# Reading the weight columns of each product as four quarters by turns

## The chip, the cores and the metric

The program runs on one core of one Trainium2 chip. The metric is the device time of one execution in microseconds (us). A core has a matrix engine (PE, whose loads of the stationary operand are shown apart as PEld), a vector engine (DVE), a scalar engine (ACT), GpSimd (POOL) and a queue engine (SP), which work side by side and wait for each other by semaphores.

## The reference

Two transformer-like blocks of depth one are computed one after the other on 256 rows of 2048 numbers, all in float32. Cut to its large products:

```
h    = rmsnorm(x) * (1 + sc_a) + sh_a          # sc_a, sh_a, ... = silu(c) @ w_ada + b_ada
proj = h @ w_in                                # 2048 x 6144; then rope, dilated and differential attention
x    = x + gt_a * rmsnorm(mix @ w_out)         # 2048 x 2048
f    = (silu(h @ w_gate) * (h @ w_up)) @ w_down
x    = x + gt_f * rmsnorm(f)
# second block
proj = h @ w_in_2 + b_in_2                     # mLSTM in chunks, a causal convolution, gates
merged = sigmoid(g_a) * (h_a @ w_proj_a_2) + sigmoid(g_b) * (h_b @ w_proj_b_2)
x    = x + gate * (merged @ w_out_2)
```

## The kernel before

The rows of the activations are the stationary operand, two tiles of 128 rows, transposed beforehand so that the contraction lies on the partitions. The weights stream through as the moving operand. They are arranged on the host into chunks of 128 partitions x 2048 float32, each a contiguous row per partition. The SP queue brings one chunk per DMA into RAW. The stages are named first (w_in and w_out), ffn (w_gate and w_up), down (w_down) and second (all weights of the second block). Chunks of the two modulation matrices (w_mod) are mixed in between; they are not used as matrix products, DVE multiplies and sums them (L1638).

Float32 products of full precision are built from three cheaper ones. A chunk is used in two halves of 1024 columns. For each half ACT rounds RAW to the type fp32r and writes it to HI (L669), DVE writes the rest, RAW minus HI, to LO (L1628). The activations stand likewise as XH and XL. PE then sums XH x HI, XL x HI and XH x LO in PSUM. A product with operands of type fp32r passes once through the array ("one-pass product"); a product with plain float32 operands is shown in the trace as two records, each of which takes longer. Every one-pass product of the weights has a stationary operand of 128 x 128 and 512 moving columns:

- `products` (L1181 with HI, L1186 with LO) serves ffn and down: for each half 8 products with HI and 4 with LO.
- `narrow_high` (L1197, L1198) and `narrow_low` (L1206) serve first and second: again 8 and 4 for a half.
- `narrow_direct` (L1221) takes some halves of the first stage as plain float32, from WHOLE, so that neither HI nor LO is needed. These halves are chosen by `is_direct`.

HI and LO have four slots of one half each (HLS = 4). PE's last product of a half raises half_used, which allows ACT to write that slot again. The order of work on each engine is written out by hand; the queues hold to it.

At the start, PE has little to do. It runs idle products on a square of ones (`run_warm`, L1282), 22 behind the products that spread c over the partitions (L1289), and 14 behind the first transposes (L1261), before the first real products of the weights (L1221). Results of these idle products are overwritten.

Of the kernel before, what the change touches and what calls it, by code (L numbers as in the profile page):

```python
# [22 lines left out]
F32 = mybir.dt.float32  # L23
# [7 lines left out]
P = 128  # L31
# [9 lines left out]
NKF = D_FF // P  # L41
# [12 lines left out]
HLS = 4  # L54
# [23 lines left out]
W_IN_COLS = [3072, 4096, 3584, 4608, 5120, 5632, 0, 1024, 512, 1536, 2048, 2560]  # L78
# [19 lines left out]
def first_half(h):  # L98

    if h < 8 * EARLY:  # L100
        n, g = divmod(h, EARLY)
    else:
        g, n = divmod(h, 8)
    return g, n, n == 0, n == 7
# [6 lines left out]
def is_direct(h):  # L111
    if h >= 8 * EARLY:
        return False
    g, n, *_ = first_half(h)
    return g in DIRECT and n < DIRECT_PAIRS
# [248 lines left out]
def build(nc, x, c_rows, pos_cols, smalls, lambda_q1, lambda_k1, lambda_q2, lambda_k2,  # L364
# [4 lines left out]
    with ctx:  # L369
# [8 lines left out]
        PS = ctx.enter_context(nc.psum_tensor("PS", [P, 8, 512], F32))  # L378
        RAW = sb("RAW", [P, RAWS, 2048])
        HI = sb("HI", [P, HLS, 1024], F32R)  # L380
        LO = sb("LO", [P, HLS, 1024], F32R)
# [127 lines left out]
        s = namedtuple("Semaphores", names)(*[sem(n) for n in names])  # L509
# [28 lines left out]
        def as_it_is(h):  # L538

            n, g = divmod(h, EARLY)  # L540
            return WHOLE[:, (n * len(DIRECT) + DIRECT.index(g)) % 4, :]

        def bank_of(g):
            return 2 * (g % 2)
# [628 lines left out]
        def _(pe):  # L1173
            def products(ready, slot, slot_k, bank_of, first, last, rows=range(NT)):

                pe.wait_ge(s.hi_ready, ready)
                for u in rows:
                    xh, xl = (v[:, slot_k, u * P:(u + 1) * P] for v in (XH, XL))
                    for x in (xh, xl):
                        for cc in range(2):  # L1180
                            pe.matmul(PS[:, bank_of(u, cc), :], x, HI[:, slot, cc * 512:(cc + 1) * 512],  # L1181
                                      start=first and x is xh, stop=False)
                pe.wait_ge(s.lo_ready, ready)
                for u in rows:
                    for cc in range(2):
                        m = pe.matmul(PS[:, bank_of(u, cc), :], XH[:, slot_k, u * P:(u + 1) * P],  # L1186
                                      LO[:, slot, cc * 512:(cc + 1) * 512], start=False, stop=last)
                return m

            def narrow_high(sec, h, n, bank, start, us):  # L1190

                pe.wait_ge(s.hi_ready, sec.half(0, h) + 1)
                for kk in range(2):
                    hi = HI[:, h % HLS, kk * 512:(kk + 1) * 512]
                    for u in us:
                        rows = slice(u * P, (u + 1) * P)
                        pe.matmul(PS[:, bank + u, :], XH[:, 2 * n + kk, rows], hi, start=start and kk == 0, stop=False)  # L1197
                        pe.matmul(PS[:, bank + u, :], XL[:, 2 * n + kk, rows], hi, start=False, stop=False)  # L1198

            def narrow_low(sec, h, n, bank, stop, us):  # L1200

                pe.wait_ge(s.lo_ready, sec.half(0, h) + 1)
                for kk in range(2):
                    lo = LO[:, h % HLS, kk * 512:(kk + 1) * 512]
                    for u in us:
                        m = pe.matmul(PS[:, bank + u, :], XH[:, 2 * n + kk, u * P:(u + 1) * P], lo, start=False,  # L1206
                                      stop=stop and kk == 1)
                if 1 in us:
                    m.then_inc(s.half_used, 1)
                return m  # L1210
# [68 lines left out]
            def run_warm(bank, count):  # L1279

                for _ in range(count):
                    pe.matmul(PS[:, bank, 0:P], ONES_SQUARE, ONES_SQUARE, start=True, stop=True)  # L1282

            pe.wait_ge(s.dve_chain, 2)
            run_warm(7, 9)
            pe.wait_ge(s.c_silu, 1)
            for n in range(2):
                for b in (2 * n, 2 * n + 1):
                    m = pe.matmul(PS[:, b, :], ONES_SQUARE, C_ROW[:, 512 * b:512 * b + 512], start=True, stop=True)  # L1289
                m.then_inc(s.c_spread, 1)  # L1290
            run_warm(7, 22)
            pe.wait_ge(s.small_in, 16)
            pe.wait_ge(s.cact_ready, 1)
            pe.wait_ge(s.xn_0, 1)
# [3 lines left out]
            for k in range(NK):  # L1298
                m = turn(1, k)
                if k % 4 == 3:  # L1300
                    m.then_inc(s.src_t, 1)
            pe.wait_ge(s.xt_out, 1)
            run_warm(0, 14)
            pe.wait_ge(s.xt_out, 4)

            used = [0]
# [125 lines left out]
            for h in range(sec.n_halves):  # L1432
                if h < 96:
                    g, n, start, stop = first_half(h)
                    bank = first_bank(g)
# [12 lines left out]
                else:  # L1448
                    g, k = W_OUT_CHUNKS[(h - 96) // 2]
                    n = 2 * k + h % 2  # L1450
                    bank = 2 if h // 4 in (25, 27, 29) else 0
                    start, stop = h in (96, 100, 104, 116, 120), h in (99, 111, 115, 119, 127)
# [12 lines left out]
                if h == sec.n_halves - 4:  # L1465

                    for i in range(4):
                        m = narrow(sec, h + i, n + i, bank, False, i == 3, (0,))
# [29 lines left out]
            for it in sec.items:  # L1498
                if it["kind"] != "W":
                    continue  # L1500
                g, k = it["what"]
                q = g % 2
                for hf in range(2):
                    h = it["half"] + hf
# [94 lines left out]
            for h in range(2, HALVES_2):  # L1599
                g, n = divmod(h, 8)  # L1600
# [6 lines left out]
                if h == HALVES_2 - 4:  # L1607

                    for i in range(4):
                        m = narrow(sec, h + i, n + i, bank_of(g), False, i == 3, (0,))  # L1610
# [6 lines left out]
        def _(dve):  # L1617
            link = chain(dve, s.dve_chain)
# [213 lines left out]
            link(dve.memset(ONES_SQUARE, 1.0))  # L1832
            link(dve.memset(C_ROW, 0.0))
            link(dve.memset(GATE_COL, 0.0))
            dve.wait_ge(s.cact_ready, 1)
            sec = secs["first"]

# [246 lines left out]
            for it in sec.items:  # L2084
# [14 lines left out]
                for hf in range(2):  # L2099
                    h = it["half"] + hf  # L2100
# [15 lines left out]
            for it in sec.items:  # L2116
# [3 lines left out]
                g = it["what"][0]  # L2120
# [314 lines left out]
def laid_out(inputs):  # L2435

    w = {name: np.asarray(inputs[name])[0] for name in ("w_ada", "w_ada_2", "w_in", "w_out", "w_gate", "w_up", "w_down", "w_in_2",
                                                        "w_proj_a_2", "w_proj_b_2", "w_out_2")}

    def rows(v, k, n):  # L2440

        return v[k * P:(k + n) * P].reshape(n, P, -1).transpose(1, 0, 2)

    def chunks(pieces):
        return np.stack([np.concatenate(p, axis=2).reshape(P, 2048) for p in pieces])


    turned = [w[name].T.reshape(-1, P, D) for name in ("w_ada", "w_ada_2")]

    def in_turn(a, b):  # L2450

        return np.concatenate([np.stack([a[0:NK], a[NK:2 * NK]], axis=1).reshape(-1, *a.shape[1:]), a[2 * NK:], b])

    def first():
        for n in range(16):
            yield [np.concatenate([rows(w["w_in"][:, W_IN_COLS[g]:W_IN_COLS[g] + 512], 2 * k, 2)
                                   for g, k, *_ in (first_half(2 * n), first_half(2 * n + 1))], axis=1)]
        for n in range(16, 48):
            g, k, _, _ = first_half(2 * n)
            yield [rows(w["w_in"][:, W_IN_COLS[g]:W_IN_COLS[g] + 512], 2 * k, 4)]  # L2460
        for g, k in W_OUT_CHUNKS:
            yield [rows(w["w_out"][:, 512 * g:512 * g + 512], 4 * k, 4)]

    def ffn():
        for g in range(11):
            for k in range(0, NK, 2):
                yield [rows(w[name][:, 512 * g:512 * g + 512], k, 2) for name in ("w_gate", "w_up")]

    def second():
        for g in range(GROUPS_2):  # L2470
            name, at = source_of(g)
            for k in range(0, NK, 4):
                yield [rows(w[name][:, at:at + 512], k, 4)]

    def columns(*vectors):
        return np.concatenate([np.asarray(v).reshape(-1, P).T for v in vectors], axis=1)

    b_ada, b_ada_2 = (np.asarray(inputs[name])[0].reshape(-1, P) for name in ("b_ada", "b_ada_2"))
    return {"w_mod": in_turn(*turned), "w_first": chunks(first()), "w_ffn": chunks(ffn()),
            "w_down": w["w_down"].reshape(NKF, P, 2048), "w_second": chunks(second()),  # L2480
            "w_gates": rows(w["w_in_2"][:, GATES_AT:GATES_AT + 16], 0, NK).reshape(P, 16 * NK),
            "b_gates": np.asarray(inputs["b_in_2"])[0, GATES_AT:GATES_AT + 16].reshape(16, 1),
            "c_rows": np.concatenate([np.asarray(inputs[n]).reshape(1, D) for n in ("c", "c_2")]), "pos_cols": np.asarray(inputs["positions"]).reshape(NT, P).T,
            "smalls": np.concatenate([columns(*(inputs[n] for n in ("g_pre_attn", "g_pre_ffn", "norm1_w_2", "conv_w_2", "headnorm_w_2", "g_out_a",
                                                  "g_subln_b", "g_post_attn", "g_post_ffn"))),
                                      in_turn(b_ada, b_ada_2).T, np.eye(P), np.repeat(inverse_frequencies(), P, axis=0)],
                                     axis=1).astype(np.float32)}
# [37 lines left out]
```

## Time and profile before

| | us |
|---|---|
| median of 2 runs | 2366.81 (2366.06 to 2367.56) |
| profiled execution, first to last instruction (span) | 2365.2 |
| median less the span: what lies around it | 1.6 |
| PE busy | 2335.2 (99% of the span) |
| DVE busy | 1816.7 (77%) |
| ACT busy | 1121.5 (47%) |

The profiled execution is given by its span alone, so the sums are made on the span and 1.6 us is added. A busy share says how much of the span an engine had an instruction in work; PE's records overlap, since a product's record reaches from its entry to the end of its results, and the next product enters before that. The distance from one start to the next is what a product costs in a row of them.

### The profile page before, as it was taken

The numbers are of one execution on the slowest core, as the hardware profiler recorded it, in microseconds if no ns is written. First come the engines' busy times: TensorE is split into PE (matmuls) and PEld (weight loads), VectorE is DVE, ScalarE is ACT, GpSimd is POOL, SyncE is SP. The second block draws the span as 40 slices with busy tenths as digits, with TensorE's granted clock in tenths as the row PEclk, the third lists the DMA queues.
The fourth block names the chain that finished last, engine by engine and source line by source line (L and its number), as shares of the span: only waits on it lengthen the run. The fifth ranks groups of instructions, "written<-read, shape, count | busy, mean of one in ns | idle before, by whom it ended". The sixth has DMA issues, their size and how long they took to land.

```text
span 2365.2 us, 26320 instructions
## 1 busy us (share of the span) xinstructions
PE 2335.2 (99%) x10346; PEld 1891.5 (80%) x10346; DVE 1816.7 (77%) x2447; ACT 1121.5 (47%) x1473; POOL 14.8 (1%) x31
## 2 busy tenths in 40 slices
PE   8999999999999999999999999999999999999998
PEld 5377788788888888888878888888888888888887
DVE  6788988888888888978575577997877795555775
ACT  5355676554434444444464334444345544444453
POOL 0000000000000000000000000000000000000000
PEclk9999999999999999999999999999999999999999
DMA  9987889887788777888646555555555556555553
GB/s 398 420 294 282 309 320 336 305 320 284 282 305 307 281 280 279 313 333 318 248 157 213 199 191 195 192 194 206 204 206 204 200 203 251 204 196 192 184 195 124
DMA packets 87758, 598.48 MB, mean 253 GB/s; under 512 B 10145, under 2 KB 10209, under 8 KB 16593
## 3 DMA queue, kind: packets, MB, share of 16 engines
q1 hardware_dynamic: 85538, 588.95, 68.7%
q0 software_dynamic: 1664, 7.19, 0.9%
q8 instruction: 82, 1.34, 0.2%
q10 hardware_dynamic: 432, 0.66, 0.1%
q14 instruction: 42, 0.34, 0.0%
HBM read 594.62 MB, written 2.13 MB: 252 GB/s over the span
## 4 chain that ended last, share of the span: by engine, by line
PE 90%; DVE 4%; DMA 4%; ACT 1%; issue 1%; DVEq 0%; ACTq 0%
PE PS L1181 19%; PE PS L1197 19%; PE PS L1198 19%; PE PS L1206 19%; PE PS L1186 10%; DMA RAW<-in_w_mod 2%; DVE RAW L1638 2%; DMA RAW<-in_w_first 1%; DVE LO L1628 1%; PE PS L1333 1%; PE PS L1552 0%; DVE X L1719 0%; DMA RAW<-in_w_ffn 0%; PE PS L1322 0%; ACT HI L669 0%
## 5 line engine op out<-in xcount | busy, mean ns | idle before, releaser
L669 ACT ACTIVATE HI<-RAW 128x1024 fp32r<-128x1024 f32 x784 | 828.7, 1059 | 1101.2 <-PE PS L1206 695.2
L1628 DVE TENSOR_TENSOR LO<-RAW,HI 128x1024 fp32r<-128x1024 f32 x784 | 957.4, 1224 | 462.3 <-ACT HI L669 458.5
L1197 PE MATMUL PS<-HI,XH 128*128 128x512 f32 x2080 | 821.8, 395 | 2.8 <-ACT HI L669 1.9
L1198 PE MATMUL PS<-HI,XL 128*128 128x512 f32 x2080 | 810.5, 390 | 0.0
L1206 PE MATMUL PS<-LO,XH 128*128 128x512 f32 x2080 | 558.4, 389 | 1.8 <-DVE LO L1628 1.8
L1197 PEld LDWEIGHTS PS<-HI,XH 128*128 128x128 f32 x2080 | 390.5, 188 | 87.4 <-DVE XL L1900 3.0
L1206 PEld LDWEIGHTS PS<-LO,XH 128*128 128x128 f32 x2080 | 390.2, 188 | 84.6 <-DVE LO L1628 2.9
L1198 PEld LDWEIGHTS PS<-HI,XL 128*128 128x128 f32 x2080 | 390.7, 188 | 78.9
L1181 PE MATMUL PS<-HI,XH 128*128 128x512 f32 x1056 | 325.9, 390 | 1.7 <-DVE XL L1742 1.1
L1181 PE MATMUL PS<-HI,XL 128*128 128x512 f32 x1056 | 325.2, 389 | 0.0
L1186 PE MATMUL PS<-LO,XH 128*128 128x512 f32 x1056 | 283.9, 389 | 0.0
L1638 DVE CUSTOM_DVE_ANT_0 RAW<-RAW,BIAS 128x2048 f32<-128x2048 f32 x96 | 219.3, 2288 | 31.9 <-DMA RAW<-in_w_mod 24.1
L1670 DVE STREAM_TRANSPOSE R<-R 32x256 f32<-32x256 f32 (+1 forms) x608 | 230.7, 379 | 12.7
L1181 PEld LDWEIGHTS PS<-HI,XH 128*128 128x128 f32 x1056 | 197.6, 188 | 43.1 <-DVE XL L1742 1.8
L1181 PEld LDWEIGHTS PS<-HI,XL 128*128 128x128 f32 x1056 | 198.1, 188 | 41.4
L1186 PEld LDWEIGHTS PS<-LO,XH 128*128 128x128 f32 x1056 | 198.1, 188 | 41.4 <-DVE LO L1628 0.2
L1638 DVE CUSTOM_DVE_ANT_0 RAW<-RAW,R 128x2048 f32<-128x2048 f32 x48 | 109.9, 2289 | 0.5
L1221 PE MATMUL PS<-R 128*128 128x512 f32 x192 | 86.9, 607 | 8.5 <-ACT R L666 5.2
L1221 PEld LDWEIGHTS PS<-R 128*128 128x128 f32 x192 | 36.2, 193 | 58.5 <-issue 51.9
L666 ACT ACTIVATE R<-RAW 128x1024 f32<-128x1024 f32 x24 | 24.1, 1048 | 49.2 <-DMA RAW<-in_w_first 49.2
L2321 DVE TENSOR_TENSOR R<-PS,BIAS 128x1024 f32<-128x1024 f32 x24 | 29.2, 1217 | 0.0
L727 ACT ACTIVATE R<-PS,MOD,SCALE 128x256 f32<-128x256 f32 (+1 forms) x38 | 17.9, 521 | 4.4 <-PE PS L1270 4.3
(263 smaller groups left out, 886.9 us busy)
## 6 DMA issues: line engine op xcount, KB each, us to landing
RAW<-in_w_second SPq DMA_DIRECT2D x208, 1024.0 KB, 4.9
RAW<-in_w_mod SPq DMA_DIRECT2D x144, 1024.0 KB, 5.6
RAW<-in_w_ffn SPq DMA_DIRECT2D x88, 1024.0 KB, 4.9
RAW<-in_w_first SPq DMA_DIRECT2D x64, 1024.0 KB, 5.3
RAW<-in_w_down SPq DMA_DIRECT2D x44, 1024.0 KB, 5.0
BIAS<-in_b_in SPq DMA_DIRECT2D x40, 256.0 KB, 5.1
R<-mod_rows POOLq DMA_DIRECT2D x3, 1024.0 KB, 7.9
X<-in_x SPq DMA_DIRECT2D x2, 1024.0 KB, 8.7
```

Source lines behind the costliest of these rows:

```text
L666: act.activation(as_it_is(h), whole, ACT.Copy).then_inc(s.hi_ready, 1)
L669: act.activation(HI[:, (it["half"] + hf) % HLS, :], whole, ACT.Copy).then_inc(s.hi_ready, 1)
L1181: pe.matmul(PS[:, bank_of(u, cc), :], x, HI[:, slot, cc * 512:(cc + 1) * 512], start=first and x is xh, stop=False)
L1186: m = pe.matmul(PS[:, bank_of(u, cc), :], XH[:, slot_k, u * P:(u + 1) * P], LO[:, slot, cc * 512:(cc + 1) * 512], start=False, stop=last)
L1197: pe.matmul(PS[:, bank + u, :], XH[:, 2 * n + kk, rows], hi, start=start and kk == 0, stop=False)
L1198: pe.matmul(PS[:, bank + u, :], XL[:, 2 * n + kk, rows], hi, start=False, stop=False)
L1206: m = pe.matmul(PS[:, bank + u, :], XH[:, 2 * n + kk, u * P:(u + 1) * P], lo, start=False, stop=stop and kk == 1)
L1221: m = pe.matmul(PS[:, bank + u, :], XT[:, 2 * n + kk, u * P:(u + 1) * P], as_it_is(h)[:, kk * 512:(kk + 1) * 512], start=start and kk == 0 ...
L1628: dve.tensor_tensor(LO[:, slot, :], RAW[:, it["slot"], hf * 1024:(hf + 1) * 1024], HI[:, slot, :].bitcast(F32), ALU.subtract).then_inc(s.l ...
L1638: dve.tensor_tensor_reduce(w, w, C_ROW if a < ADA_OF_C else C_ROW_2, 1.0, 0.0, ALU.mult, ALU.add, MOD[:, a:a + 1]).then_inc(s.ada_step, 1)
L1670: m = dve.transpose(columns(b, a), rows(a, b))
L2321: dve.tensor_tensor(dst, y, bias, ALU.add).then_inc(s.group_out, 1)
```

## The change

1. On the host, each group of 512 columns of the weights that are read by one-pass products is arranged anew (`by_fours`): columns 0, 4, 8, ..., 508 come first, then 1, 5, 9, ..., then 2, 6, ..., then 3, 7, .... The halves that `narrow_direct` reads stay as they were. Sizes and number of the DMAs are the same, and so is the work of ACT and DVE on them, element by element.
2. In `products`, `narrow_high` and `narrow_low` PE reads the 512 moving columns through `by_turns`: the first element of each of the four quarters of 128, then the second of each, and so on. Within a partition consecutive reads lie 512 bytes apart, where they lay 4 bytes apart. Since the two permutations undo each other, PSUM receives the columns in their true order.
3. The 22 idle products at first are replaced by 20 one-pass products on HI slot 3 filled with ones (`first_warm`), and the 14 by 16 others (`second_warm`). They read their moving operand in several strided orders; four of the 16 are on plain float32. A memset of that slot on DVE is added for them, and PE waits for it.

```diff
+        def by_turns(v):
+            return v.rearrange("p (a b) -> p b a", a=4)
...
-                            pe.matmul(PS[:, bank_of(u, cc), :], x, HI[:, slot, cc * 512:(cc + 1) * 512],
+                            pe.matmul(PS[:, bank_of(u, cc), :], x, by_turns(HI[:, slot, cc * 512:(cc + 1) * 512]),
                                       start=first and x is xh, stop=False)
...
-                                      LO[:, slot, cc * 512:(cc + 1) * 512], start=False, stop=last)
+                                      by_turns(LO[:, slot, cc * 512:(cc + 1) * 512]), start=False, stop=last)
...
-                    hi = HI[:, h % HLS, kk * 512:(kk + 1) * 512]
+                    hi = by_turns(HI[:, h % HLS, kk * 512:(kk + 1) * 512])
...
-                    lo = LO[:, h % HLS, kk * 512:(kk + 1) * 512]
+                    lo = by_turns(LO[:, h % HLS, kk * 512:(kk + 1) * 512])
...
+            def warm(m, n, count, a, b, bank=7):
+                for _ in range(count):
+                    pe.matmul(PS[0:m, bank, 0:n], a, b, start=True, stop=True)
+
+            def first_warm():
+                v = HI[:, 3, :]
+                x = v[:, 0:P]
+                warm(P, 512, 4, x, v[:, 0:512].rearrange("p (a b) -> p b a", a=4))
+                warm(P, 512, 4, x, v[:, 0:512].rearrange("p (a b) -> p b a", a=8))
+                warm(P, 512, 4, x, v.rearrange("p (a b) -> p b a", a=2)[:, 0:256, :])
+                warm(P, 256, 4, x, v[:, 0:256].rearrange("p (a b) -> p b a", a=2))
+                warm(P, 512, 4, x, by_turns(v[:, 0:512]))
+
+            def second_warm():
+                v = HI[:, 3, :]
+                x = v[:, 0:P]
+                warm(P, 512, 4, x, v[:, 0:512].rearrange("p (a b c) -> p b a c", a=2, c=2), 0)
+                warm(P, 512, 4, x.bitcast(F32), by_turns(v[:, 0:512]).bitcast(F32), 0)
+                warm(P, 512, 4, x, v[:, 0:512].rearrange("p (a b) -> p b a", a=64), 0)
+                warm(P, 512, 4, x, by_turns(v[:, 0:512]), 0)
...
-            run_warm(7, 22)
+            pe.wait_ge(s.dve_chain, 5)
+            first_warm()
...
-            run_warm(0, 14)
+            second_warm()
...
             link(dve.memset(GATE_COL, 0.0))
+            link(dve.memset(HI[:, 3, :].bitcast(F32), 1.0))
...
+    def by_fours(a):
+        return a.reshape(*a.shape[:-1], -1, P, 4).swapaxes(-1, -2).reshape(a.shape)
...
-            yield [rows(w["w_out"][:, 512 * g:512 * g + 512], 4 * k, 4)]
+            yield [by_fours(rows(w["w_out"][:, 512 * g:512 * g + 512], 4 * k, 4))]
...
-            "w_down": w["w_down"].reshape(NKF, P, 2048), "w_second": chunks(second()),
+            "w_down": by_fours(w["w_down"].reshape(NKF, P, 2048)), "w_second": chunks(second()),
```

PE at the start of the program, before the change: L1282 are the idle products, L1289 spreads c, L1261 are the transposes of x, L1221 the first products of the weights.

```order
L1282 MATMUL PS<-R 128x128 x9
L1289 MATMUL PS<-BIAS,R 128x512 x4
L1282 MATMUL PS<-R 128x128 x22
L1261 MATMUL PS<-SMALLS,R 128x128 x32
L1282 MATMUL PS<-R 128x128 x14
L1221 MATMUL PS<-R 128x512 x96
```

The same place on PE in the changed kernel; there the idle products of `warm` are L1291, and the lines L1289, L1261 and L1221 have become L1317, L1265 and L1225.

```order
L1286 MATMUL PS<-R 128x128 x9
L1317 MATMUL PS<-BIAS,R 128x512 x4
L1291 MATMUL PS<-HI 128x512 x12
L1291 MATMUL PS<-HI 128x256 x4
L1291 MATMUL PS<-HI 128x512 x4
L1265 MATMUL PS<-SMALLS,R 128x128 x32
L1291 MATMUL PS<-HI 128x512 x16
L1225 MATMUL PS<-R 128x512 x96
```

Nothing else is moved: only the idle products in front of the transposes and in front of the first real products are others, and wider.

## Rows read from the trace of the kernel before

**Rows 1.** The page's head: span, and busy time of PE.

```profile
span 2365.2 us, 26320 instructions
...
PE 2335.2 (99%) x10346; PEld 1891.5 (80%) x10346; DVE 1816.7 (77%) x2447; ACT 1121.5 (47%) x1473; POOL 14.8 (1%) x31
```

**Rows 2.** The chain that ended last, by line, shares of the span.

```profile
by line: PE PS L1181 19.5%; PE PS L1197 19.3%; PE PS L1198 19.1%; PE PS L1206 19.1%; PE PS L1186 9.7%; DMA RAW<-in_w_mod 2.2%; DVE RAW L1638 1.5%; DMA RAW<-in_w_first 1.3%; DVE LO L1628 0.7%; PE PS L1333 0.6%; issue 0.5%; PE PS L1552 0.4%; 
```

**Rows 3.** Waits: engine, line, waited for, us in total, times, longest.

```profile
ACT HI L669 <- PE PS L1206: 695.2, 445, 2.9
```

**Rows 4.** Groups of PE's products, shapes apart: busy us, mean ns, idle before.

```profile
L1197 PE MATMUL PS<-HI,XH 128*128 128x512 f32 x2080 | 821.8, 395 | 2.8 <-ACT HI L669 1.9 <-DVE XL L1742 1.0
L1198 PE MATMUL PS<-HI,XL 128*128 128x512 f32 x2080 | 810.5, 390 | 0.0
L1206 PE MATMUL PS<-LO,XH 128*128 128x512 f32 x2080 | 558.4, 389 | 1.8 <-DVE LO L1628 1.8
L1181 PE MATMUL PS<-HI,XH 128*128 128x512 f32 x1056 | 325.9, 390 | 1.7 <-DVE XL L1742 1.1 <-issue 0.6
L1181 PE MATMUL PS<-HI,XL 128*128 128x512 f32 x1056 | 325.2, 389 | 0.0
L1186 PE MATMUL PS<-LO,XH 128*128 128x512 f32 x1056 | 283.9, 389 | 0.0
```

**Rows 5.** The chain in stage down: start us, us, what.

```profile
992.35 1.81 PE PS L1181 x8
994.16 0.91 PE PS L1186 x4
995.07 1.81 PE PS L1181 x8
```

**Rows 6.** Windows: us, busy of PE, PEld, DVE, ACT, POOL, then PEclk, DMA share, GB/s.

```profile
990.00:1000.00 10.00, 10.00 (x46) 8.29 (x45) 9.82 (x13) 4.58 (x6) 0.00 (x0) 1.00 0.94 350
1700.00:1710.00 10.00, 10.00 (x46) 8.29 (x45) 8.65 (x12) 4.43 (x5) 0.00 (x0) 1.00 0.62 210
```

**Rows 7.** The chain in stage second.

```profile
1702.37 0.91 PE PS L1206 x4
```

**Rows 8.** Timeline of PE, one-pass products of 256 columns, 16 stationary columns.

```profile
1226.12 0.28 PE L1525 MATMUL PS<-XH,WIFH 128*16 128x256 f32 x1
...
1226.69 0.28 PE L1525 MATMUL PS<-XH,WIFL 128*16 128x256 f32 x1
1226.81 0.39 PE L1197 MATMUL PS<-HI,XH 128*128 128x512 f32 x1
```

**Rows 9.** Timeline of PEld beside plain float32 products of 512 columns.

```profile
28.72 0.34 PEld L1221 LDWEIGHTS PS<-R 128*128 128x128 f32 x1 [0.52 <-issue]
29.57 0.34 PEld L1221 LDWEIGHTS PS<-R 128*128 128x128 f32 x1 [0.52 <-issue]
...
31.43 0.19 PEld L1221 LDWEIGHTS PS<-R 128*128 128x128 f32 x1 [0.24 <-ACT R L666]
31.86 0.19 PEld L1221 LDWEIGHTS PS<-R 128*128 128x128 f32 x1 [0.24 <-issue]
```

**Rows 10.** Windows of the granted clock, columns as in rows 6.

```profile
27.20:30.70 3.50, 3.50 (x6) 1.44 (x5) 2.68 (x4) 0.45 (x1) 0.00 (x0) 0.51 1.00 424
30.70:34.00 3.30, 3.30 (x8) 1.40 (x8) 1.26 (x1) 1.55 (x2) 0.00 (x0) 1.00 1.02 432
```

**Rows 11.** Windows of longer stretches, columns as in rows 6.

```profile
130.00:290.00 160.00, 157.69 (x739) 125.76 (x738) 142.89 (x262) 92.33 (x202) 1.08 (x2) 1.00 0.80 290
290.00:440.00 150.00, 149.45 (x728) 125.11 (x727) 131.89 (x179) 96.88 (x207) 0.00 (x0) 1.00 0.90 332
760.00:1040.00 280.00, 280.00 (x1237) 231.84 (x1236) 237.40 (x273) 121.12 (x129) 0.00 (x0) 1.00 0.80 293
```

**Rows 12.** Timeline of the start, DVE and PE.

```profile
3.46 0.09 DVE L1834 MEMSET SMALL<- 128x32 f32 x1
...
9.65 5.07 PE L1282 MATMUL PS<-R 128*128 128x128 f32 x44
...
11.02 2.29 DVE L1638 CUSTOM_DVE_ANT_0 RAW<-RAW,BIAS 128x2048 f32<-128x2048 f32 x1 [7.47 <-ACT BIAS L749]
...
15.29 1.94 PE L1261 MATMUL PS<-SMALLS,R 128*128 128x128 f32 x16 [0.56 <-DVE R L1849]
...
20.03 3.37 PE L1282 MATMUL PS<-R 128*128 128x128 f32 x28
```

**Rows 13.** Timeline of PE, its next work behind those idle products.

```profile
26.66 3.98 PE L1221 MATMUL PS<-R 128*128 128x512 f32 x5 [3.26 <-ACT XH L784]
```

More of the change, by code:

```diff
@@ L2452, in in_turn @@
         return np.concatenate([np.stack([a[0:NK], a[NK:2 * NK]], axis=1).reshape(-1, *a.shape[1:]), a[2 * NK:], b])
+    def by_fours(a):
+        return a.reshape(*a.shape[:-1], -1, P, 4).swapaxes(-1, -2).reshape(a.shape)
     def first():
         for n in range(16):
-            yield [np.concatenate([rows(w["w_in"][:, W_IN_COLS[g]:W_IN_COLS[g] + 512], 2 * k, 2)
-                                   for g, k, *_ in (first_half(2 * n), first_half(2 * n + 1))], axis=1)]
+            halves = []
+            for h in (2 * n, 2 * n + 1):
+                g, k, *_ = first_half(h)
+                piece = rows(w["w_in"][:, W_IN_COLS[g]:W_IN_COLS[g] + 512], 2 * k, 2)
+                halves.append(piece if is_direct(h) else by_fours(piece))
+            yield [np.concatenate(halves, axis=1)]
         for n in range(16, 48):
             g, k, _, _ = first_half(2 * n)
-            yield [rows(w["w_in"][:, W_IN_COLS[g]:W_IN_COLS[g] + 512], 2 * k, 4)]
+            yield [by_fours(rows(w["w_in"][:, W_IN_COLS[g]:W_IN_COLS[g] + 512], 2 * k, 4))]
         for g, k in W_OUT_CHUNKS:
-            yield [rows(w["w_out"][:, 512 * g:512 * g + 512], 4 * k, 4)]
+            yield [by_fours(rows(w["w_out"][:, 512 * g:512 * g + 512], 4 * k, 4))]
     def ffn():
@@ L2466, in ffn @@
             for k in range(0, NK, 2):
-                yield [rows(w[name][:, 512 * g:512 * g + 512], k, 2) for name in ("w_gate", "w_up")]
+                yield [by_fours(rows(w[name][:, 512 * g:512 * g + 512], k, 2)) for name in ("w_gate", "w_up")]
     def second():
@@ L2472, in second @@
             for k in range(0, NK, 4):
-                yield [rows(w[name][:, at:at + 512], k, 4)]
+                yield [by_fours(rows(w[name][:, at:at + 512], k, 4))]
     def columns(*vectors):
```

## The prediction

> **What bounds the kernel now.** I read the page's head first: PE is busy for 2335.2 of 2365.2 us [rows 1]. A busy share alone doesn't tell that an engine sets the time, so the chain of waits comes second. By line it is L1181, L1197, L1198, L1206 and L1186, together 86.7% of the span [rows 2]. These are exactly the lines whose moving operand the change reads otherwise. Seen from the other side, ACT spends 695.2 us waiting for PE to release a slot of HI [rows 3], which is what a producer does when the consumer is the bound.
>
> Next comes what one product costs in a row of them, the distance between starts and not the mean of 389 ns in the groups [rows 4], which holds the pipeline too. The chain has 8 products in 1.81 us and 4 in 0.91 us [rows 5]: 1.81 / 8 = 226.3 ns, and one half of 12 products takes 995.07 − 992.35 = 2.72 us, so 226.7 ns each. The granted clock is 1.00 there [rows 6], the 2.4 GHz level, and at one column per cycle 512 columns would take 512 / 2.4 = 213.3 ns. So 13.3 ns of each are over, one part in 16.
>
> **Where the 13.3 ns come from** decides the forecast, and four rows narrow it.
> - It is not traffic: the DMA share is 0.94 in one stretch and 0.62 in the other [rows 6], and the price of 4 products is 0.91 us in both [rows 5, 7].
> - It is no fixed cost for an instruction. The one-pass products of 256 columns start 6 in 1226.81 − 1226.12 = 0.69 us [rows 8], 115 ns each against 106.7 ns of columns: 8 ns over. With half the columns well over half of the excess stays, so I take a part by column and a little by instruction.
> - It is not the load of the stationary operand: those products load 16 columns instead of 128 and have the excess all the same [rows 8].
> - It is gone when columns are taken at half the rate. A record of a plain float32 product of 512 columns takes 31.86 − 31.43 = 0.43 us at the high clock [rows 9, 10], about 2 x 213.3 = 426.7 ns plus some 2 ns. Had the loss been one in 16 there as well, it would be 453 ns.
>
> So what is lost is lost while PE takes 4-byte columns from neighbouring addresses at one per cycle. Either the reader stumbles on neighbouring addresses (one cycle lost for each 64 bytes), which another order may avoid, or it can't deliver more than this of 4-byte elements in any order. No product of the kernel before reads its moving operand with a step, so no row tells which; the price of the new reading has to be bounded from both sides.
>
> **The change, part by part.**
>
> *The reading by turns.* It concerns 3 x 2080 + 3 x 1056 = 9408 products [rows 4]. On the chain they make 86.7% of 2365.2 = 2050.6 us [rows 2], which is 2050.6 / 0.2267 = 9046 of them; the others lie beside other work, mostly in the first 130 us. The best price is the bare 213.3 ns plus the some 2 ns that a float32 record has over its columns [rows 9], an estimate of 215.3 ns. That saves 11.4 ns x 9046 = 103 us, and 107 us if all 9408 count. The lower end without any fixed cost is 13.3 x 9408 = 125 us saved. The worst near price is that of a record that takes columns at half the rate, 0.43 us [rows 9]: 0.203 x 9408 = 1910 us lost. I take the end at 215.3 ns. The reason is the last of the four rows: the loss follows the full rate over neighbouring addresses, not the number of columns, and by turns each of four streams is read at a quarter of the rate. It is a judgement, and the price of being wrong is large.
>
> The Trainium skill has a rule that speaks against this: "Advanced Engine Details and Errata", section "SBUF Cachelines", says that memory is read in lines of 16 bytes, that at least two hits on a line are needed to cover its latency, and that a different line at each access is penalised. By turns every read is in another line than the one before. No row of this trace shows a strided read by PE, so the rule is neither confirmed nor refuted; what it would do is the first rival below. The same skill's "TensorE: Matmul & The Clock Gate", section "Back-to-back issue gap", gives the distance of isolated products as N / 2.4 + 2.5 ns, 215.8 ns for 512 columns; the trace has 226.7. An estimate by that page would save 10.9 x 9046 = 99 us, about what my sum has.
>
> *What the faster PE runs into.* With 215.3 ns a half takes 2.58 us instead of 2.72. DVE is busy for 142.89 of 160 us from 130 on, 131.89 of 150 from 290 on and 237.40 of 280 us in 760 to 1040 [rows 11]. If these stretches shrink by some 4 to 5%, its share goes to 94%, 92% and 89%. It stays below PE, but its work comes in blocks of 2.29 us (L1638) [rows 12] and LO must be there in time. The DMA share in 290 to 440 goes from 0.90 to 0.94. I book 2 us of new waits, between 0 and 12 us.
>
> *ACT and DVE on HI and LO, and the DMAs.* Same sizes, contiguous on their side: nothing.
>
> *The memset on DVE.* It stands behind the one at 3.46 us; DVE then idles 7.47 us until 11.02 for ACT's BIAS [rows 12]. A memset of 1024 columns lies in there. Cost nothing; PE's new wait for it is over before 9.65, where the idle products begin.
>
> *The first idle products.* Before: 44 records in 5.07 us, from 9.65 to 14.7, and the transposes begin at 15.29, since they wait for DVE [rows 12]. Now 16 of 512 and 4 of 256 columns: at 0.215 and 0.11 us that is 3.9 us, done at 13.6. At half the rate 16 x 0.43 + 4 x 0.21 = 7.7 us, done at 17.4, 2 us late.
>
> *The second idle products.* Before: 3.37 us from 20.03 [rows 12]. Now 12 x 0.215 + 8 records of 0.43 (four plain float32 products) = 6.0 us, done at 26.1; PE's next work waits for ACT until 26.66 [rows 13]. Cost nothing, 0.6 us to spare. At half the rate it ends at 28.6, 2 us late. They also fill the 3.26 us of idle time [rows 13], after which the granted clock fell to 0.51 from 27.2 to 30.7 [rows 10], the 1.2 GHz level, where a record took 0.85 us instead of 0.43 [rows 9]. Four records could gain 1.7 us, but this part of the chain goes through the DMAs of w_mod and w_first (3.5% of the span in rows 2), so I book nothing.
>
> Sum: 2365.2 − 103 + 2 = 2264 us of span, plus the 1.6 us around it as the median has it: **2266 us**, 4.3% less.
>
> **The rivals.**
> 1. *Every read pays for a new line (slower).* The place is the read of the moving operand in all 9408 products. If the reader fetches a line for each element and gets a fetch only every other cycle, a product takes 0.43 us as in rows 9, and the time is 2366.8 + 1910 = about 4275 us. For it: neighbouring columns are taken at almost one per cycle, so a fetch serves several, and a stride throws this away. Against it: nothing in the rows but the reasoning above. It decides from a price of 226.7 + 5 ns on, since 2% of 2366.8, 47 us, over 9408 products is 5.0 ns. Chance 0.20, with all prices between that and half the rate.
> 2. *The excess is the rate of the 4-byte reader in any order (same).* Then each product stays at 226.7 ns, and only the start moves: 2364 to 2371 us. For it: 1 in 16 is so regular that it could be a ratio of rates. Against it: nothing that a row shows. Chance 0.13.
> 3. *Half the excess goes.* 6.7 ns x 9046 = 60 us: 2307 us, still faster by 2.5%. Chance 0.12.
> 4. *DVE or DMA takes over* in the stretches to 1040 us: the products are at 215 ns but 10 to 25 us come back: 2276 to 2291 us. The blocks on DVE speak for it, the shares below 94% against it. Chance 0.08.
>
> **How the numbers follow.** My forecast has 0.47, rivals 3 and 4 have 0.20 and end on the same side: faster by over 2% has 0.67. Within 2% is rival 2, 0.13. Slower by over 2% is rival 1, 0.20. (2%, 47 us, is about what a measurement of this kernel can tell from no change.) The range holds forecast and rivals 2 to 4 and leaves out rival 1: its low end is the bare columns, 2366.8 − 125 = 2242, a little drawn in to 2246 since no row shows PE without any cost for an instruction; its high end is rival 2 with the start 4 us late, 2371. The faster cases alone would lie in 2246 to 2310.
>
> **What the profile of the changed kernel would show.** The chain in the stages ffn and down should have 8 products in 1.72 us instead of 1.81, at an unchanged granted clock of 1.00; 1.81 speaks for rival 2, 3.4 for rival 1. The mean of the product groups should fall from 389 to about 378 ns. The waits of ACT's HI for PE should shrink, and the chain should still be PE, with no waits of PE for LO above a few us; if those sum to 10 us or more, rival 4 holds. The new idle products are all by strided reads, and the distances of their starts show at once which stride costs what. I would be wrong by the size of the step if the reader, not the order, sets one in 16, and wrong by far if an order of other lines halves the rate.

## The result and the profile after

| | us |
|---|---|
| before, median of 2 runs | 2366.81 (2366.06 to 2367.56) |
| after, median of 2 runs | 2880.62 (2880.17 to 2881.07) |
| ratio after / before | 1.2168, 95% interval 1.2145 to 1.2191 |
| span of the profiled execution after | 2879.1 |

The change makes the kernel 21.7% slower. (One execution among the experiments, 2928.55 us of the kernel with quarters by turns in two stages, had a granted clock of 0.752 where its other one had 0.998, and stands in no comparison.) The head of the page after, which answers to [rows 1]:

```profile
span 2879.1 us, 26257 instructions
...
PE 2861.3 (99%) x10314; PEld 1929.2 (67%) x10314; DVE 1823.0 (63%) x2448; ACT 1124.7 (39%) x1473; POOL 14.8 (1%) x31
```

DVE and ACT are busy for nearly as many us as before (6.3 and 3.2 more); PE's busy time has grown by 526 us. The chain that ended last, by line (L1185, L1190 are the products of ffn and down, L1201, L1202, L1210 those of first and second), against [rows 2]:

```profile
by line: PE PS L1185 20.7%; PE PS L1201 20.5%; PE PS L1210 20.4%; PE PS L1202 20.4%; PE PS L1190 10.4%; DMA RAW<-in_w_mod 1.8%; DVE RAW L1667 0.9%; DMA RAW<-in_w_first 0.5%; PE PS L1362 0.5%; PE PS L1581 0.4%; PE PS L1274 0.2%; PE PS L1351 
```

The five lines together hold 92.4% of 2879.1 = 2660 us, where they held 2051. The rest of the chain has fallen from 315 to 219 us: pieces of DMA, DVE and issue that were links of it before now lie beside the longer work of PE. 610 − 96 = 514 us is the difference of the spans. The price of one product is read from the chain at the end of stage down (start us, us, what), which answers to [rows 5]:

```profile
1180.87 1.13 PE PS L1190 x4
1182.00 2.27 PE PS L1185 x8
1184.27 1.13 PE PS L1190 x4
1185.40 2.27 PE PS L1185 x8
```

A half of 12 products takes 1185.40 − 1182.00 = 3.40 us, 283.3 ns each, where it took 226.7. A window (columns as in rows 6) shows the same granted clock as before:

```profile
1180.00:1190.00 10.00, 10.00 (x37) 6.77 (x36) 6.89 (x8) 3.49 (x5) 0.00 (x0) 1.00 0.55 179
```

And the groups by shape, against [rows 4]: the mean of a record is 454 and 450 ns instead of 395 and 389.

```profile
L1201 PE MATMUL PS<-HI,XH 128*128 128x512 f32 x2080 | 944.2, 454 | 0.8 <-ACT HI L673 0.4 <-DVE XL L1771 0.3
...
L1210 PE MATMUL PS<-LO,XH 128*128 128x512 f32 x2080 | 676.9, 450 | 1.0 <-DVE LO L1657 1.0
```

9408 products at 56.6 ns more would be 533 us; 19 us less are measured. The start, which is bound by DMAs, took up none of them, since the first product of the weights that reads by turns starts at 118.7 us (the same one at 119.1 before). Some 14.5 of the 19 us belong to the first 1600 products: they take 506.7 us (118.7 to 625.4) where they took 430.6 (119.1 to 549.7), which is 76.1 us more and not 90.6. The profile lists PE as idle for 1.4 us in that stretch, for 6.9 before, so part of it is waiting that has gone; the rest stays open.

The start, PE's timeline, against [rows 12, 13]: the records of the second idle products end only at 30.77 us, and PE's next work starts at 30.60, where it started at 26.66.

```profile
8.58 6.07 PE L1291 MATMUL PS<-HI 128*128 128x512 f32 x20
14.62 1.94 PE L1265 MATMUL PS<-SMALLS,R 128*128 128x128 f32 x16
...
19.35 11.42 PE L1291 MATMUL PS<-HI 128*128 128x512 f32 x20
30.60 1.88 PE L1225 MATMUL PS<-R 128*128 128x512 f32 x4
```

The first idle products already told what the experiments below separate. The starts of their records lie 279 to 284 ns apart with four streams at 512 bytes, 482 to 487 with eight, 216 with two streams at 2048 bytes. (A stream is one of the places from which the columns are taken by turns; its distance is that to the next stream.)

### The profile page after: what moved, and what is told of

The parts are those of the page before. It is cut to its first block, busy times and chain, and to the rows that moved or that the text cites. A ratio compares the mean times of both kernels' runs of the same rounds, so it can differ in the third digit from the quotient of the medians.

```text
span 2879.1 us, 26257 instructions
## 1 busy us (share of the span) xinstructions
PE 2861.3 (99%) x10314; PEld 1929.2 (67%) x10314; DVE 1823.0 (63%) x2448; ACT 1124.7 (39%) x1473; POOL 14.8 (1%) x31
## 4 chain that ended last, share of the span: by engine, by line
PE 95%; DMA 2%; DVE 2%; ACT 1%; issue 0%; DVEq 0%; ACTq 0%
PE PS L1185 21%; PE PS L1201 20%; PE PS L1210 20%; PE PS L1202 20%; PE PS L1190 10%; DMA RAW<-in_w_mod 2%; DVE RAW L1667 1%; DMA RAW<-in_w_first 1%; PE PS L1362 0%; PE PS L1581 0%; PE PS L1274 0%; PE PS L1351 0%; PE PS L1554 0%; PE PS L1413 0%; PE PS L1383 0%; PE PS L1393 0%
## 5 line engine op out<-in xcount | busy, mean ns | idle before, releaser
L1201 PE MATMUL PS<-HI,XH 128*128 128x512 f32 x2080 | 944.2, 454 | 0.8 <-ACT HI L673 0.4
L1202 PE MATMUL PS<-HI,XL 128*128 128x512 f32 x2080 | 934.1, 449 | 0.0
L1210 PE MATMUL PS<-LO,XH 128*128 128x512 f32 x2080 | 676.9, 450 | 1.0 <-DVE LO L1657 1.0
L1210 PEld LDWEIGHTS PS<-LO,XH 128*128 128x128 f32 x2080 | 398.7, 192 | 190.5 <-DVE LO L1657 1.5
L1201 PEld LDWEIGHTS PS<-HI,XH 128*128 128x128 f32 x2080 | 398.5, 192 | 185.2 <-ACT HI L673 2.0
L1202 PEld LDWEIGHTS PS<-HI,XL 128*128 128x128 f32 x2080 | 398.6, 192 | 179.7
L1185 PE MATMUL PS<-HI,XH 128*128 128x512 f32 x1056 | 388.2, 451 | 1.2 <-DVE XL L1771 1.1
L1185 PE MATMUL PS<-HI,XL 128*128 128x512 f32 x1056 | 387.6, 451 | 0.0
L1190 PE MATMUL PS<-LO,XH 128*128 128x512 f32 x1056 | 345.1, 451 | 0.0
L1190 PEld LDWEIGHTS PS<-LO,XH 128*128 128x128 f32 x1056 | 202.7, 192 | 96.5
L1185 PEld LDWEIGHTS PS<-HI,XL 128*128 128x128 f32 x1056 | 202.7, 192 | 96.3
L1185 PEld LDWEIGHTS PS<-HI,XH 128*128 128x128 f32 x1056 | 202.1, 192 | 96.6 <-DVE XL L1771 1.3
L1225 PE MATMUL PS<-R 128*128 128x512 f32 x192 | 84.6, 596 | 3.1 <-ACT R L670 3.1
L1225 PEld LDWEIGHTS PS<-R 128*128 128x128 f32 x192 | 35.8, 190 | 51.5 <-issue 45.7
```

The lines of the kernel that those rows point to most:

```text
L1185: pe.matmul(PS[:, bank_of(u, cc), :], x, by_turns(HI[:, slot, cc * 512:(cc + 1) * 512]), start=first and x is xh, stop=False)
L1225: m = pe.matmul(PS[:, bank + u, :], XT[:, 2 * n + kk, u * P:(u + 1) * P], as_it_is(h)[:, kk * 512:(kk + 1) * 512], start=start and kk == 0 ...
```

## The experiments

### The arrangement alone

```diff
         def by_turns(v):
-            return v.rearrange("p (a b) -> p b a", a=4)
+            return v
```

The idle products keep their order of reading, four streams included.

> The weights keep the changed arrangement on the host, but PE reads them from neighbouring addresses as before; the new idle products stay. The columns therefore reach PSUM in the order of the arrangement, so everything behind the first product is computed on permuted columns; the amount of work is the same. Theory A (the order of PE's reads alone sets the price of a product): 226.7 ns for each of the 9408 products, and a time of 2364 to 2371 us, that of the kernel before with another start. Theory B (the arrangement or what comes with it, the DMAs or ACT and DVE on it, costs part of the 514 us): between 2371 and 2880 us.

Measured: 2365.78 us, ratio to before 0.9997 (0.9987 to 1.0007). (Ratios are to executions of the kernel before made together with the experiment; their median is 2366.55 us here.) Theory A. Host arrangement, DMAs, ACT and DVE on arranged columns and the new idle products cost nothing; all of the 514 us lie in PE's order of reading.

### The idle products alone

```diff
-            run_warm(7, 22)
+            pe.wait_ge(s.dve_chain, 5)
+            first_warm()
...
-            run_warm(0, 14)
+            second_warm()
...
+            link(dve.memset(HI[:, 3, :].bitcast(F32), 1.0))
```

> The kernel before with the changed kernel's idle products and memset alone. They end at 30.6 us instead of 23.4, and in the changed kernel the next work of PE began 3.9 us later than before. Theory A (the start is hidden behind the DMAs of the first weights): within 2364 to 2371 us. Theory C (the later start is passed on whole or grows): 2371 us or more.

Measured: 2365.48 us, ratio 0.9995 (0.9985 to 1.0006), although PE's first real product starts at 31.11 us:

```profile
31.11 1.45 PE L1225 MATMUL PS<-R 128*128 128x512 f32 x3
```

A start that is 4 us late is hidden: the first one-pass product of the weights starts at 119.0 us, as before (119.1). That the DMAs set the pace in between is argued from the chain, not tested alone; the DMA share of the first 130 us before is 1.00.

### Quarters by turns in two stages only

```diff
-                            pe.matmul(PS[:, bank_of(u, cc), :], x, HI[:, slot, cc * 512:(cc + 1) * 512],
+                            pe.matmul(PS[:, bank_of(u, cc), :], x, by_turns(HI[:, slot, cc * 512:(cc + 1) * 512]),
...
-                                      LO[:, slot, cc * 512:(cc + 1) * 512], start=False, stop=last)
+                                      by_turns(LO[:, slot, cc * 512:(cc + 1) * 512]), start=False, stop=last)
...
-                yield [rows(w[name][:, 512 * g:512 * g + 512], k, 2) for name in ("w_gate", "w_up")]
+                yield [by_fours(rows(w[name][:, 512 * g:512 * g + 512], k, 2)) for name in ("w_gate", "w_up")]
...
-            "w_down": w["w_down"].reshape(NKF, P, 2048), "w_second": chunks(second()),
+            "w_down": by_fours(w["w_down"].reshape(NKF, P, 2048)), "w_second": chunks(second()),
```

Both products are those of `products`; `narrow_high`, `narrow_low` and their weights are as in the kernel before.

> One part of the change alone: quarters by turns (and the arrangement for them) only in the products of the stages ffn and down, 3 x 1056 = 3168 of the 9408; all others and the idle products as before. Theory A (a fixed price for each product that reads by turns): 3168 x (283.3 - 226.7) = 179 us more than before, 2546 us. Theory D (the loss comes from PE's reads being in the way of others in one stage, or is not the same in all stages): clearly more or less than a third of the 514 us, outside 2530 to 2560.

Measured: 2542.38 us, within what theory A said, but one execution gives no interval. So it was repeated:

> The same kernel as in the run with quarters by turns in ffn and down only, with more executions for the interval. Theory A: 2546 us, with 2540 to 2550 as what its first profile showed; theory D: outside 2530 to 2560.

Measured: 2543.96 us (2542.16 to 2546.31), ratio 1.0749 (1.0731 to 1.0767). That is 177 us more than before, for 3168 products at 56.6 ns = 179 us. The groups of this kernel show both prices side by side, the turned ones at 451 ns of record, the others at 389 to 395 as before:

```profile
L1201 PE MATMUL PS<-HI,XH 128*128 128x512 f32 x2080 | 821.8, 395 | 3.9 <-ACT HI L673 3.3 <-DVE XL L1746 0.5
...
L1185 PE MATMUL PS<-HI,XL 128*128 128x512 f32 x1056 | 387.6, 451 | 0.0
```

Theory A: a fixed price per product, paid almost in full (177 of 179 us), since PE is the bound. Theory D falls.

### Halves by turns instead of quarters

```diff
         def by_turns(v):
-            return v.rearrange("p (a b) -> p b a", a=4)
+            return v.rearrange("p (a b) -> p b a", a=2)
...
     def by_fours(a):
-        return a.reshape(*a.shape[:-1], -1, P, 4).swapaxes(-1, -2).reshape(a.shape)
+        return a.reshape(*a.shape[:-1], -1, 2 * P, 2).swapaxes(-1, -2).reshape(a.shape)
```

> Two halves by turns instead of four quarters: each 512 columns are arranged as the even ones and then the odd ones, and read with 1024 bytes between the two streams; the idle products are those of the kernel before. In the changed kernel's start, idle products that read two streams 2048 bytes apart began 216 ns apart, and those with four streams 283 ns. Theory A1 (up to two alternating streams are read at the full rate): 216 ns for each product, 2366.8 - 9408 x 10.7 ns = 2266 us if nothing else becomes late, 2266 to 2280 with some waits for DVE. Theory A2 (every read in another place than the one before costs, and the 216 ns were an effect of ones as data or of the 2048 bytes): 250 to 283 ns, 2586 to 2880 us.

Measured: 2268.8 us (2267.39 to 2270.34), ratio to before 0.9586 (0.9570 to 0.9602). This version beats both kernels. Its chain in stage down:

```profile
900.65 1.73 PE PS L1185 x8
902.38 0.86 PE PS L1190 x4
903.24 1.73 PE PS L1185 x8
```

(903.24 − 900.65) / 12 = 215.8 ns. Theory A1 holds with the real data and a distance of 1024 bytes. 9408 x 10.9 ns = 102.5 us would have given 2264 us; 4.7 us of that are not gained. By the profiles 4.5 us are missing from the first 1600 products: these take 417.7 us (118.5 to 536.2) instead of 430.6, 12.9 us less and not 17.4, and PE is idle for 10.4 us there, for 6.9 before. In the chain by line the five product lines hold 78.0% instead of 86.7%, and DVE's LO (L1656) has grown from 0.7% in [rows 2] to 3.6%. That isn't time lost, since PE waits for LO for 1.5 us in all; it suggests that DVE and PE now finish closer together (DVE is busy for 147.42 of 160 us from 130 us on, for 142.89 before).

```profile
by line: PE PS L1185 19.3%; PE PS L1201 16.4%; PE PS L1210 16.4%; PE PS L1202 16.3%; PE PS L1190 9.6%; DVE LO L1656 3.6%; DMA RAW<-in_w_mod 2.3%; DVE R L1698 2.1%; DVE RAW L1666 2.0%; issue 1.5%; DMA RAW<-in_w_first 1.5%; ACT HI L673 0.6%; 
```

### Which order costs what

Three kernels are the kernel before with groups of six idle products at the start, on ones, each group on its own line:

```diff
-            run_warm(7, 22)
+            pe.wait_ge(s.dve_chain, 5)
+            FLAT = HI[:].rearrange("p a b -> p (a b)")
...
+            for _ in range(6):
+                pe.matmul(PS[:, 7, :], FLAT[:, 3072:3200], FLAT[:, 0:512].rearrange("p (a b) -> p b a", a=2), start=True, stop=True)
...
+            for _ in range(6):
+                pe.matmul(PS[:, 7, :], FLAT[:, 3072:3200], FLAT[:, 0:528].rearrange("p (a b) -> p b a", a=4)[:, 0:128, :], start=True, stop=True)
...
+            link(dve.memset(HI[:].bitcast(F32), 1.0))
```

> The kernel before, with its 22 first idle products replaced by 20 groups of 6 one-pass products of 512 columns on ones, each group on a line of its own, each with another order of reading; the time itself is not of interest (some 30 to 40 us more at the start), the distances of the starts are. Theory P (PE's reader takes consecutive elements alternately in two ways, and each way is fast while its own reads go on at the next address): two streams 216 ns at any distance (1024, 1028, 1040, 2048 bytes), four streams slow at any distance (about 283 ns), pairs from two halves slow (about 335 ns), groups of 16 from two halves about as neighbouring addresses, 227 ns. Theory Q (reads collide by their address, since 512 bytes is a power of two): four streams at 528 bytes fall towards 216 to 227 ns, and eight at 272 bytes fall well under the 486 ns of eight at 256. Theory R (what counts is that a read is in another line than the one before): two streams would be as slow as four, and a step of 8 bytes faster than one of 16.

The three kernels took 2409.07, 2391.38 and 2392.78 us, one execution each; only the distances below are used. The timeline of PE; a group's price is the next group's start less its own, divided by six (by twelve for plain float32, with two records a product):

```profile
10.37 1.46 PE L1296 MATMUL PS<-HI 128*128 128x512 f32 x6
11.67 1.46 PE L1298 MATMUL PS<-HI 128*128 128x512 f32 x6
12.96 1.46 PE L1300 MATMUL PS<-HI 128*128 128x512 f32 x6
...
15.55 1.83 PE L1304 MATMUL PS<-HI 128*128 128x512 f32 x6
17.21 1.80 PE L1306 MATMUL PS<-HI 128*128 128x512 f32 x6
18.84 1.79 PE L1308 MATMUL PS<-HI 128*128 128x512 f32 x6
20.47 1.86 PE L1310 MATMUL PS<-HI 128*128 128x512 f32 x6
22.17 3.18 PE L1312 MATMUL PS<-HI 128*128 128x512 f32 x6
25.17 2.82 PE L1314 MATMUL PS<-HI 128*128 128x512 f32 x6
27.81 2.92 PE L1316 MATMUL PS<-HI 128*128 128x512 f32 x6
30.55 2.94 PE L1318 MATMUL PS<-HI 128*128 128x512 f32 x6
33.31 2.16 PE L1320 MATMUL PS<-HI 128*128 128x512 f32 x6
35.29 1.68 PE L1322 MATMUL PS<-HI 128*128 128x512 f32 x6
36.81 1.61 PE L1324 MATMUL PS<-HI 128*128 128x512 f32 x6
38.26 5.31 PE L1326 MATMUL PS<-HI 128*128 128x512 f32 x12
43.41 6.64 PE L1328 MATMUL PS<-HI 128*128 128x512 f32 x12
49.88 10.64 PE L1330 MATMUL PS<-HI 128*128 128x512 f32 x12
```

| lines | order of reading, one-pass columns of 4 bytes | ns |
|---|---|---|
| L1296, L1298 | two streams at 1024, 2048 bytes | 217, 215 |
| L1300 and the group behind it | two streams at 1028 and 1040 bytes, (15.55 − 12.96) / 12 | 216 |
| L1304, L1306, L1308, L1310 | four streams at 512, 528, 576, 2048 bytes | 277, 272, 272, 283 |
| L1312, L1314 | eight streams at 256, 272 bytes | 500, 440 |
| L1316, L1318 | one stream with a step of 8, of 16 bytes | 457, 460 |
| L1320, L1322, L1324 | two halves by turns in pairs, fours, sixteens | 330, 253, 242 |
| L1326, L1328 | a record of plain float32, neighbours, two halves | 429, 539 |
| L1330 | the same, four quarters (between the starts within the group) | 873 |

Theory P comes through for two streams at any distance, for four and for pairs; sixteens cost 242 where it said 227. Theory Q falls as the cause: four streams at 528 and 576 bytes cost 272 ns, far from 216 to 227. A part depends on the distance all the same: at 512 and 2048 bytes the last starts of a group lie 280 to 283 ns apart, at 528 and 576 bytes 271 to 272, which is 11 of the 56.6 ns; with eight streams the distance is worth 60 ns. Theory R falls twice, since two streams never read twice in a row from one line of 16 bytes and are the fastest, and since a step of 8 bytes is no faster than one of 16.

> The kernel before with 18 other groups of 6 idle products at the start, each on a line of its own; again only the distances of the starts are of interest. Theory P (consecutive elements go by turns to two readers, and a reader is slowed when its own next address lies 16 bytes or more on) says: two streams that each advance by 8 bytes 227 to 235 ns, as neighbouring addresses; two streams that advance by 16 bytes about 455; a step of 12 bytes about 455; pairs of neighbours at every 16 bytes about 455; four neighbours at every 32 bytes about 231; six streams over 280 ns for 512 columns. Theory S (a product is at 216 ns whenever two streams alternate, whatever their steps) says 216 for both stepped pairs of streams. Theory R2 (what counts is how many of the reads in a row share a line of 16 bytes, two being enough) says pairs of neighbours at every 16 bytes at 227 to 250. Neighbouring addresses with 16 stationary columns: 227 to 235 with any theory, and four streams with 16 stationary columns 272 to 284. Elements of 2 bytes from neighbouring addresses: 216 ns, and under theory P four streams of them stay under 284.

```profile
11.00 1.57 PE L1297 MATMUL PS<-HI 128*128 128x512 f32 x6
12.41 1.53 PE L1299 MATMUL PS<-HI 128*128 128x512 f32 x6
13.77 2.88 PE L1301 MATMUL PS<-HI 128*128 128x512 f32 x6
16.47 1.57 PE L1303 MATMUL PS<-HI 128*128 128x384 f32 x6
17.88 2.88 PE L1305 MATMUL PS<-HI 128*128 128x512 f32 x6
20.57 2.89 PE L1307 MATMUL PS<-HI 128*128 128x512 f32 x6
23.28 1.57 PE L1309 MATMUL PS<-HI 128*128 128x512 f32 x6
24.69 0.88 PE L1311 MATMUL PS<-HI 128*128 128x256 f32 x6
...
30.43 3.07 PE L1321 MATMUL PS<-HI 128*128 128x512 bf16 x6
33.34 5.35 PE L1323 MATMUL PS<-HI 128*128 128x512 bf16 x6
38.51 2.62 PE L1325 MATMUL PS<-HI 128*128 128x512 bf16 x6
```

Neighbours (L1297, from an address 4 bytes on) are at 235 ns on ones. Two streams that each advance by 8 bytes (L1299): 227. Two that advance by 16 (L1301): 450. A step of 12 bytes (L1305): 448. Pairs of neighbours at every 16 bytes (L1307): 452. Fours at every 32 bytes (L1309): 235. The last five are near what theory P says, though its words would make fours at every 32 bytes dearer, as every second read of a reader there goes 24 bytes on; S says 216 for L1299 and R2 says 227 to 250 for L1307, and both fall. With 16 stationary columns the starts of neighbours lie 229 to 238 ns apart and those of four streams 279 to 284, about as with 128. Six streams (L1303) take 235 ns for 384 columns, 313 for 512. Where P was wrong is the element of 2 bytes (bf16 in the rows): two halves by turns (L1321) take 485 ns and four (L1323) 862, while neighbours of 2 bytes start 216 ns apart.

> The kernel before with 13 other groups of 6 idle products at the start; only the distances of the starts are of interest. Open is why four streams of one-pass columns take 272 to 284 ns and not the 452 ns of two streams that each advance by 16 bytes, although with four streams either reader changes its place at each read. Theory K (a reader keeps more than one place of 16 bytes, and pays when the place it needs was not kept): four streams that advance by 8 bytes cost more than 284 ns and those that advance by 16 bytes about 452. Theory N (nothing is kept, a change between two far places is merely cheaper than the next place in a row): all three of them 272 to 284 ns. Four streams in groups of four neighbours: about 250 as with two. Pairs from two streams that advance by 16 bytes: 452 under K, about 330 under N. Elements of 2 bytes, from two halves in pairs: 216 to 250 if two neighbouring ones are read as one of 4 bytes, about 484 if not. Plain float32 with a step of 8 bytes: 429 to 900, no theory.

```profile
10.37 1.84 PE L1297 MATMUL PS<-HI 128*128 128x512 f32 x6
12.04 2.16 PE L1299 MATMUL PS<-HI 128*128 128x512 f32 x6
14.03 3.07 PE L1301 MATMUL PS<-HI 128*128 128x512 f32 x6
16.91 1.81 PE L1303 MATMUL PS<-HI 128*128 128x512 f32 x6
18.55 1.47 PE L1305 MATMUL PS<-HI 128*128 128x512 f32 x6
19.86 3.07 PE L1307 MATMUL PS<-HI 128*128 128x512 f32 x6
22.74 1.82 PE L1309 MATMUL PS<-HI 128*128 128x512 bf16 x6
24.40 1.46 PE L1311 MATMUL PS<-HI 128*128 128x512 bf16 x6
```

Four streams that advance by 4, 8 and 16 bytes (L1297, L1299, L1301) take 278, 332 and 480 ns; pairs from two streams that advance by 16 bytes (L1307) 480. So theory N falls, and K, that places are kept, is the better one; K's 452 is too low by 28. Four streams in fours (L1303): 273, where I had 250. Elements of 2 bytes from two halves: 277 in pairs (L1309), which neither of the two expectations has; in groups of eight (L1311) their records start 215 to 217 ns apart. Plain float32 with a step of 8 bytes takes 451 ns a record, with a step of 16 bytes about 900.

**One count that orders these prices.** Take the columns in the order of reading, split them into the two series of theory P (0, 2, 4, ... and 1, 3, 5, ...), and count how many reads in a row a series makes within the same 16 bytes:

| reads in a row | orders of one-pass columns of 4 bytes | ns |
|---|---|---|
| 4 | two streams | 215 to 217 |
| 2 | neighbours; two streams that advance by 8 bytes; fours at every 32 bytes | 227 to 235 |
| 2, then another place | sixteens and fours from two halves, fours from four streams | 242, 253, 273 |
| 1, one other place between, 4 reads in all | four streams | 272 to 283 |
| 1, one other place between, 2 in all | pairs from two halves; four streams that advance by 8 bytes | 330, 332 |
| 1 in all | steps of 8, 12, 16 bytes; two streams by 16 bytes; pairs at every 16 bytes | 448 to 460 |
| 1 in all, other places between | four streams by 16 bytes; pairs from two streams by 16 bytes | 480 |
| 1, three other places between, 4 in all | eight streams | 440 to 500 |

The sharpest pair is two streams that advance by 8 bytes (227) against pairs of neighbours at every 16 bytes (452): both make two reads in each 16 bytes, but only in the first do both fall to the same series. The count was found after the runs, on ones, for columns of 4 bytes, and no further run tested it; no run looks inside PE's reader. Elements of 2 bytes don't follow it: two halves have eight reads in a row by this count and cost 485 ns.

## Why the prediction was wrong

**What held.** That PE is the bound and that these five lines are its share; that the price per product is the whole matter; that its excess of 13.3 ns hangs on the order in which 4-byte columns are taken (halves by turns take it away, 215.8 ns against the 215.3 that I had as the best end; but it isn't bound to neighbouring addresses, since two streams that advance by 8 bytes have it too, at 227 ns); that arrangement, memset and start cost nothing (ratios 0.9997 and 0.9995); that only a few us of a faster PE's gain are lost again (4.7, where I booked 2 and allowed 12).

**The step that failed** is the choice of the value: "I take the end at 215.3 ns", with the reason that "by turns each of four streams is read at a quarter of the rate". It treated any order that avoids neighbours as equally good. What the runs showed in its place is 283.3 ns for four streams. The stepped streams speak for a reader that cares where alternate reads lie: columns 0, 2, 4, ... of the order of reading among themselves, and 1, 3, 5, ... among themselves. With two streams each of these two series goes on by 4 bytes and costs nothing; with neighbours by 8 bytes (227 to 235 ns); with a new stretch of 16 bytes at each read, about 450 ns. With four streams each series jumps between two far quarters at each read, which costs 283.3 ns. That the order of reading alone costs the 514 us is shown; that there are two such series is inferred from the prices. My four rows could not tell two streams from four, and I had no row with a stride at all.

**The rival** that came true is the first, every read pays, in its direction and in being linear in the products. Its size, half the rate for each read and 4275 us, was too large: 56.6 instead of 203 ns were added. I left the rival out of the range with a chance of 0.20, while the choice between the ends rested on judgement alone.

**A count** was read wrongly. The 9046 products were taken from the chain's share, the others to lie beside other work, mostly in the first 130 us; but only 48 of the 9408 start before 130 us in the kernel before, and the chain after holds nearly all of them (2660 us at 283.3 ns are 9390). With 9408 the best end would have saved 107 us, still inside the range.

**A smaller step** was off too. The second idle products were to end at 26.1 or at worst 28.6; they ended at 30.77, mainly because a plain float32 record with four streams takes 0.86 to 0.87 us rather than the 0.43 that I gave it in both cases. It cost nothing. The fall of the clock to 0.51 [rows 10] is gone with the idle time (1.00 from 27.2 to 30.7 us), which gained nothing measurable either.

**On the page that spoke against it.** The Trainium skill, "Advanced Engine Details and Errata", section "SBUF Cachelines", was right that quarters by turns are penalised (283.3 ns against 226.7 here). Counted over all of PE's one-pass columns its terms don't fit: two hits in a row on a line don't help (step of 8 bytes 457 ns, pairs at every 16 bytes 452), and another line at each access is the fastest of all with two streams (215.8). Counted in each of the two series by itself, two hits on a line do divide 216 to 235 ns from about 450. The page doesn't say how PE's reads are to be counted.

## What to carry to other kernels

An unexplained excess of a few per cent in a bounding engine's price can sometimes be won back, but which access order does it has to be measured: here two streams give 4.1% and four lose 21.7%. Groups of six idle products at the start, each order on a line of its own, priced 19 orders in one execution, for 42 us more; run them before the whole kernel is turned to an order. Where a forecast has to choose between ends that lie 200 ns apart without a row for either, the far end belongs in the range.

## What the runs showed of the hardware

- One-pass columns of 4 bytes, 512 in a product: neighbours 226.7 ns in the kernel, two streams 215.8, four 283.3, at a granted clock of 1.00.
- The order that is best for one-pass columns is not for the others. A plain float32 record takes 429 ns from neighbours and 539 from two halves; elements of 2 bytes take 216 from neighbours and 485 from two halves.
- The distance of the streams matters little with two (215 to 217 ns), some 11 ns with four (272 or 283), and more with eight (500 at 256 bytes, 440 at 272). Why four streams cost 283 and not 450, and how many places are kept, is open: the prices of 278, 332 and 480 ns for four streams that advance by 4, 8 and 16 bytes speak for places being kept, and no more was tried. Neighbours cost 226.7 ns in the kernel but 227 to 238 on ones in the groups; that difference has no explanation either.
- Two reads on the same 16 bytes are cheap when columns two apart in the order of reading fall there (227 ns), and dear when adjacent ones do (452).
